# Prompt rows and v rows at other places in VectorE's order, slots of three tiles at earlier blocks

## What is computed

```
q = (x @ w_q).reshape(n, 8, 2, 128)
s1, s2 = q[:, :, 0] @ key1.T, q[:, :, 1] @ key2.T        # 128 keys each
t1, i1 = top_k(s1, 16); t2, i2 = top_k(s2, 16)
top, pos = top_k(all 256 sums t1 + t2, 16)
idx = i1 * 128 + i2 at pos; g = softmax(top)             # 16 of 16384 experts per head
a = sum(u_tab[idx] * x)                                  # one dot product per expert
out = sum(gelu(a) * g * v_tab[idx])
```

## Time and profile before

| | |
|---|---|
| median of three runs | 3657.13 us (3656.3 to 3658.6) |
| the profiled execution | 3659.94 us |
| its span, first to last instruction | 3658.1 us |
| TensorE busy | 3434.4 us, 94% of the span |
| VectorE busy | 2617.4 us, 72% |
| ScalarE, GpSimd busy | 860.4 us, 1728.9 us |
| mean granted TensorE clock | 0.965 |
| DMA | 1263 MB, 345 GB/s over the span |

### The profile page before, as it was taken

How to read it: one execution, slowest core, us unless ns; L and a number is a source line. 1 busy time by engine, 2 the same in 40 slices (tenths; PEclk the granted TensorE clock), 3 DMA queues, 4 the chain that set the end, 5 groups by cost and what they waited for, 6 DMA issues and landing times.

```text
span 3658.1 us, 38233 instructions
## 1 busy us (share of the span) xinstructions
PE 3434.4 (94%) x12478; PEld 2101.6 (57%) x12478; DVE 2617.4 (72%) x6009; ACT 860.4 (24%) x2206; POOL 1728.9 (47%) x1362
## 2 busy tenths in 40 slices
PE   6898989999889999999988988999997999999998
PEld 2555446889778444444435454478886964444443
DVE  0378777898976866666535788689988767666666
ACT  1114311147632000000021160111676310000000
POOL 2035355444635555566300643554456436556661
PEclk9898999999999999999989988999998999999999
DMA  9967588999999999999874965899999999999994
GB/s 361 329 225 264 197 308 326 379 370 370 408 387 377 390 414 413 399 414 412 333 273 153 340 205 194 306 390 375 360 382 408 349 383 401 413 414 398 413 415 170
DMA packets 413989, 1263.48 MB, mean 345 GB/s; under 512 B 36240, under 2 KB 139664, under 8 KB 370784
## 3 DMA queue, kind: packets, MB, share of 16 engines
q0 software_dynamic: 192000, 721.61, 51.0%
q1 hardware_dynamic: 171808, 514.20, 37.0%
q10 hardware_dynamic: 49984, 25.23, 2.3%
HBM read 1174.07 MB, written 86.84 MB: 345 GB/s over the span
## 4 chain that ended last, share of the span: by engine, by line
PE 66%; DVE 14%; DMA 11%; issue 3%; POOL 2%; ACT 2%; SPq 1%; ACTq 0%; DVEq 0%; POOLq 0%
PE P L975 23%; PE P L947 10%; PE P L921 6%; PE V L975 6%; PE O L975 6%; DVE late L1336 4%; PE P L772 4%; DMA gate_d<-hT 3%; PE T L959 3%; POOL ring L686 2%; PE P L755 2%; DMA ring<-in_w_mod_dram 2%; DMA ring<-in_peer_v_dram,eidx 2%; PE O L819 2%; DMA acts_d<-late 1%
## 5 line engine op out<-in xcount | busy, mean ns | idle before, releaser
L686 POOL DMA_INDIRECT ring<-in_peer_u_dram,eidx x768 | 984.3, 1282 | 1011.9 <-DVE ring L1318 644.4
L1318 DVE SCALAR_TENSOR_TENSOR ring<-ring,h 128x1024 f32<-128x1024 f32 x768 | 917.3, 1222 | 159.8 <-DMA ring<-in_peer_u_dram,eidx 152.2
L686 POOL DMA_INDIRECT ring<-in_peer_v_dram,eidx x512 | 704.7, 1376 | 621.1 <-DVE late L1336 348.4
L975 PE MATMUL P<-w_ring,area 128*128 128x512 f32 x2048 | 920.1, 592 | 3.0 <-DVE area L1519 2.2
L947 PE MATMUL P<-hT,w_ring 128*128 128x256 f32 x4096 | 920.5, 383 | 0.0
L947 PEld LDWEIGHTS P<-hT,w_ring 128*128 128x128 f32 x4096 | 777.7, 193 | 102.4
L975 PEld LDWEIGHTS P<-w_ring,area 128*128 128x128 f32 x2048 | 388.6, 190 | 493.8 <-issue 493.7
L1336 DVE SCALAR_TENSOR_TENSOR late<-ring,dots,late 128x1024 f32<-128x1024 f32 x254 | 329.1, 1296 | 55.6 <-DMA ring<-in_peer_v_dram,eidx 38.5
L1336 DVE SCALAR_TENSOR_TENSOR h<-ring,dots,h 128x1024 f32<-128x1024 f32 x254 | 325.7, 1282 | 21.1 <-DMA ring<-in_peer_v_dram,eidx 5.6
L921 PE MATMUL P<-hT,w_ring 128*128 128x128 f32 (+1 forms) x1024 | 287.7, 443 | 2.9 <-issue 2.9
L975 PE MATMUL O<-w_ring,qT 128*128 128x512 f32 x512 | 261.4, 592 | 0.0
(11 more groups left out here) (233 smaller groups left out, 3289.4 us busy)
## 6 DMA issues: line engine op xcount, KB each, us to landing
w_ring<-in_peer_uT_dram SPq DMA_DIRECT2D x128, 1024.0 KB
w_ring<-in_peer_vB_dram SPq DMA_DIRECT2D x128, 1024.0 KB
ring<-in_w_mod_dram POOLq DMA_DIRECT2D x48, 1024.0 KB, 8.2
w_ring<-in_peer_wq_dram SPq DMA_DIRECT2D x64, 512.0 KB, 5.9
h<-acts_d SPq DMA_DIRECT2D x64, 512.0 KB
w_ring<-in_w_in_dram SPq DMA_DIRECT2D x48, 512.0 KB, 3.9
area<-gate_d SPq DMA_DIRECT2D x16, 1536.0 KB
hT<-gate_d SPq DMA_DIRECT2D x16, 1536.0 KB
```

The costliest lines, as they stand in the source:

```text
L686: pool.indirect_dma_start(out=ring[:, b, :], out_offset=None, in_=tables["uv".index(phase)], in_offset=bass.IndirectOffsetOnAxis(ap=eidx[: ...
L975: mm = pe.matmul(bank[ACC[2 * t + half]][:, :], w, uv_ring[:, b // 2 % (WR // 2), b % 2, half * 512:(half + 1) * 512], start=b == 0, stop= ...
L1318: dve.scalar_tensor_tensor(ring[:, b, :], ring[:, b, :], 1.0, h2[:, k, :], ALU.mult, ALU.mult, accum_out=dots[:, k, row:row + 1]).then_inc ...
```

## The change

The prompt rows move: 38 instead of 36 after the input projection, 15 (`WAIT_ROWS`) instead of 8 before the wait for the LayerNorm rows, three instead of two after each of three tiles, and all the other 26 in one run after the last tile; none stand before the key steps. ScalarE's `gelu_dots(0)` moves from j = 7 to j = 3 and VectorE's `expert_weights(0)` from j = 7 to j = 4. The v rows in the key steps stand in three groups: 20 at j = 4, 18 at j = 8 and 18 at j = 12, 56 instead of 52. Beside the search of tile 3 stand 20 v rows (in six steps instead of twelve), to row 76 instead of 72, and 24 rows of tile 1 instead of 16. The `slT` jobs of tiles 3, 4 and 1 move from blocks 43, 75 and 101 to 33, 64 and 97. The chunks of tile 3 begin at block 37 instead of 47 at the same rate; those of tile 4 take 28 blocks from block 66 instead of 23 from 77; those of tile 1 take 20 blocks from 99 instead of 16 from 103. Beside the chunks of tile 1 stand 24 v rows instead of 28, and 12 more come after the last of them, so 16 instead of 28 are left for the v stage. ScalarE's softmax and gelu jobs move with the slots.

```diff
--- before.py
+++ after.py
@@ -57,11 +57,14 @@
 OH_BUFS = 5
 OH_AHEAD = OH_BUFS - 1
 ACT_SIDE = QUAD - 1
-PV_EARLY = 72
-IN_ROWS = 36
-OUT_ROWS = 2
-QUERY_ROWS = 52
-PV_LATE = 100
+QUERY_ROWS = {4: (0, 20), 8: (20, 38), 12: (38, 56)}
+PV_EARLY = 76
+PV_BESIDE = 100
+PV_LATE = 112
+IN_ROWS = 38
+WAIT_ROWS = 15
+OUT_ROWS = 3
+SEARCH_ROWS = 24
 V_DONE = KEYS - 1
 
 SEARCHED_EARLY = 16
@@ -101,7 +104,7 @@
 
 
 
-SLOT_BLOCKS = {43: 3, 75: 4, 101: 1}
+SLOT_BLOCKS = {33: 3, 64: 4, 97: 1}
 
 SEARCH_CHUNKS = 22
 
@@ -111,8 +114,8 @@
 def chunk_block(k, q):
 
     if k == 3:
-        return 47 + q if q < SEARCH_CHUNKS else 70 + (q - SEARCH_CHUNKS) // 2
-    first, blocks = {4: (77, 23), 1: (103, 16)}[k]
+        return 37 + q if q < SEARCH_CHUNKS else 59 + (q - SEARCH_CHUNKS) // 2
+    first, blocks = {4: (66, 28), 1: (99, 20)}[k]
     return first + blocks * q // CHUNKS
 
 
@@ -1114,7 +1117,7 @@
                                            ready(job)[:, :].rearrange("p (c n) -> p c n", c=4), ACT.Copy
                                            ).then_inc(emptied[BANK[job]], 1)
                     for j in range(2 * PH + 1):
-                        if g == "S" and j == 7:
+                        if g == "S" and j == 3:
                             gelu_dots(0)
                         if j < 2 * PH:
 
@@ -1158,11 +1161,11 @@
                                        ).then_inc(emptied[BANK[job]], 1)
                         if b == 18:
                             top_softmax(1)
-                        if b == 41:
+                        if b == 29:
                             top_softmax(3)
-                        if b == 65:
+                        if b == 55:
                             top_softmax(4)
-                        if b == 100:
+                        if b == 96:
                             gelu_dots(1)
                     elif job[0] == "slT":
                         k = job[1]
@@ -1679,7 +1682,7 @@
                     modulation("attended")
                     if latent:
 
-                        prompt_rows(GP)
+                        prompt_rows(WAIT_ROWS)
                     dve.wait_ge(rows_in, (2 * l + (gi + 1)) * 48)
                     for t in range(nt):
                         for n in range(2):
@@ -1688,36 +1691,33 @@
                         if latent and t < nt - 1:
                             prompt_rows(OUT_ROWS)
                     if latent:
-                        prompt_rows(SLOTS - IN_ROWS - 40 - GP - OUT_ROWS * (nt - 1) - 20)
+                        prompt_rows(SLOTS - IN_ROWS - 40 - WAIT_ROWS - OUT_ROWS * (nt - 1))
                     modulation("summed")
                     for j in range(2 * PH):
-                        if latent and j < 5:
-                            prompt_rows(4)
-                        if latent and j == 7:
+                        if latent and j == 4:
                             expert_weights(0)
-                        if latent and j >= 7:
-                            add_rows(0, QUERY_ROWS * (j - 7) // 9, QUERY_ROWS * (j - 6) // 9)
+                        if latent and j in QUERY_ROWS:
+                            add_rows(0, *QUERY_ROWS[j])
                         first_tile_keys(g, j)
                     for step in range(6):
                         choose(tiles[0], step)
 
                 for i in range(2 * PH + 6):
-                    if i < 12:
-                        add_rows(0, QUERY_ROWS + (PV_EARLY - QUERY_ROWS) * i // 12,
-                                 QUERY_ROWS + (PV_EARLY - QUERY_ROWS) * (i + 1) // 12)
+                    if i < 6:
+                        add_rows(0, 56 + 20 * i // 6, 56 + 20 * (i + 1) // 6)
                     else:
-                        dot_rows(1, 16 * (i - 12) // 10, 16 * (i - 11) // 10)
+                        dot_rows(1, SEARCH_ROWS * (i - 6) // 16, SEARCH_ROWS * (i - 5) // 16)
                     choosing(3, i)
                 slots_out(3)
                 for i in range(2 * PH + 6):
-                    dot_rows(1, 16 + ROWS_BESIDE * i // 22, 16 + ROWS_BESIDE * (i + 1) // 22)
+                    dot_rows(1, SEARCH_ROWS + ROWS_BESIDE * i // 22, SEARCH_ROWS + ROWS_BESIDE * (i + 1) // 22)
                     one_hots(3, i)
                     choosing(4, i)
                 slots_out(4)
                 for i in range(CHUNKS - SEARCH_CHUNKS):
                     one_hots(3, SEARCH_CHUNKS + i)
-                    dot_rows(1, 16 + ROWS_BESIDE + i, 17 + ROWS_BESIDE + i)
-                near = 16 + ROWS_BESIDE + CHUNKS - SEARCH_CHUNKS + GP
+                    dot_rows(1, SEARCH_ROWS + ROWS_BESIDE + i, SEARCH_ROWS + ROWS_BESIDE + i + 1)
+                near = SEARCH_ROWS + ROWS_BESIDE + CHUNKS - SEARCH_CHUNKS + GP
                 dot_rows(1, near - GP, near)
                 for i in range(CHUNKS):
                     one_hots(4, i)
@@ -1727,8 +1727,9 @@
                 slots_out(1)
                 for i in range(CHUNKS):
                     one_hots(1, i)
-                    add_rows(0, PV_EARLY + (PV_LATE - PV_EARLY) * i // CHUNKS,
-                             PV_EARLY + (PV_LATE - PV_EARLY) * (i + 1) // CHUNKS)
+                    add_rows(0, PV_EARLY + (PV_BESIDE - PV_EARLY) * i // CHUNKS,
+                             PV_EARLY + (PV_BESIDE - PV_EARLY) * (i + 1) // CHUNKS)
+                add_rows(0, PV_BESIDE, PV_LATE)
 
                 for b in range(KEYS):
                     weights_T(b)
```

## The result

The changed kernel takes 3729.0 us (3725.5 to 3739.9), the kernel before 3656.7 us: a ratio of 1.0216 (95% interval 1.0197 to 1.0235). Forecast were 3671 us with a range of 3634 to 3694. The sign was right, the size was not: +72 us instead of +14, outside the range and beyond the slowest of the rivals (3691). It is the fastest of four executions, so the ledger is 7 us short of the difference of the medians.

The account below looks back on a forecast made before the run. TensorE, busy 94%, was taken as the bound, with DMA traffic close behind in the u stage. +10.2 + 6.7 - 3.0 = +13.9 us on the median of 3657.1 gave 3671 us, own range 3660 to 3684, 8-in-10 range 3634 to 3694.

Parts of the forecast that it names:

- Part 1: Before the first score: two more prompt rows on VectorE's path cost 2.8 us a layer (2.3 to 3.5).
- Part 2: Wait for LN rows: seven more rows fit VectorE's waits and cost zero, or 2 us without the second wait's cover.
- Part 3: Output projection: a third row in each of three tiles makes VectorE 2.55 us later, all on TensorE's path.
- Part 4: 26-row run and gelu at j = 3: ScalarE's late query 3 stalls TensorE, 7.7 us a layer (0.2 to 18).
- starved rival: Run of 26 rows: every gather behind the ring is slow, 50.4 us instead of 40.1; 3691 us in all, chance 0.10.
- lock of the Trainium skill: Run of 26 rows: GpSimd, writing descriptors, can be locked out of a port pair for a whole VectorE instruction.
- Part 5: Slots of tile 3: VectorE has them at 766.5 us as before, so TensorE waits 25 us instead of 4.
- Part 6: Rest of the u stage behind the slots: middle values of 420.6 us (+10.2) and 424.9 us (+6.7) by layer.
- upper end: Stretch behind the slots: DMA traffic of 163.2 MB at the old rate, 427 us and 435.5 us in layer 1.
- sign of being right: Rest of the u stage: TensorE's waits at line 959 for chunks under 13 us a layer.
- Part 7: First v-stage blocks: 16 v rows beside them instead of 28 win 1.5 us a layer.
- sum: Whole kernel: +10.2 + 6.7 - 3.0 = +13.9 us, giving 3671 us.

Follow-up runs that it names:

- gelu4_wait8: Changed kernel with gelu_dots(0) at ScalarE's j = 4 instead of 3 and WAIT_ROWS 8 instead of 15: 3710.9 us, 1.0169 of the kernel before.
- gelu_at_4: Changed kernel with only gelu_dots(0) moved from ScalarE's j = 3 to j = 4: 3717.3 us, 1.0190 of the kernel before.
- search_16: Changed kernel with SEARCH_ROWS 16 instead of 24: 3724.2 us, 1.0185 of the kernel before.
- halved gathers: Tile 1's u rows behind the slots gather 512 instead of 1024 numbers per token: 3699.3 us in the changed kernel, 3604.5 us in the kernel before.
- even spread: Changed kernel with tile 3's last ten chunks one a block instead of two, tile 4's slots at block 69, its chunks in 24 blocks: 3740.4 us.
- late_rows_100: Changed kernel with PV_LATE 100 instead of 112, twelve v rows back beside the v stage's first blocks: 3724.0 us, 1.0193 of the kernel before.
- order_only: Kernel before with only the new places of slots, chunks and ScalarE's softmax and gelu jobs, no row moved: 3713.5 us, 1.0176.
- rows alone: Changed kernel with slots, chunks and ScalarE's softmax and gelu places of the kernel before, row moves kept: 3678.0 us, 1.0084.

## Why the prediction was wrong in size

**Part 1 (+2.8)** was somewhat small. The start of the output projection in layer 0 moves by 0.4 us between the two profiled executions (409.71 to 410.09), but the changed one is the earliest of eight with 38 rows: the middle ones differ by 3.9 us (409.8 and 413.7). In layer 1, from the prompt's last h2 to the projection, they differ by 3.3.

**Part 2 (0) failed.** "Their gathers come late by 1 to 3 us, which the second wait covers": they came late by 3.45, 2.02, 1.45, 1.56 and 1.00 us, 9.5 in all, and the second residual starts 6.8 us later, not 0 to 2. The wait that was to be filled was itself a wait for DMA (the LN rows), whose share was already 0.85 in that window and rises to 0.99. `gelu4_wait8` shows the cost by taking the seven rows away: 6.4 us in layer 0 of the changed kernel, 4.8 against `gelu_at_4` in both layers. That it is the sharing of the engines, and not only that 15 rows are more than the ring's eight, fits the windows but no run separates the two.

**Part 3 (+2.55)** is right: in steady state a tile of 15.17 us where TensorE's takes 14.61 or less; with Part 2 taken away the projection to T3 takes 69.81 us instead of 67.26, and the wait for the last h2 is 12.08 us (`gelu4_wait8`), against 12 forecast. With Part 2 it is 14.07.

**Part 4 (+7.7, 6.8 of it stall)** is right in kind and nearly in size: a stall of 5.54 us at the predicted line, the run of 26 rows in 40.8 us (40.1 forecast from before), ScalarE idle before the gelu; T3 to the u stage grows by 6.3 us. The starved rival (50.4 us for the run) does not hold: the rows came at the old pace. So the lock of the Trainium skill (SBUF — State Buffer, "SBUF: two separate sides") does not make every gather of this run slow: from 487 to 527 us they take 0.93 to 1.99 us on GpSimd. The u stage starts at 626.4, 15.7 us later (13 forecast). The fix of one step gives 8.4 us back.

**Part 5 (slots at 766.5, a wait of 25 us)** had the mechanism and missed the time: 779.9 and 35.9 us. VectorE's wait at keys 3 is 25.09 us (26 forecast) and the pair search starts at 651.0 (648.0 forecast, from a T3 4 us earlier). Then "from there to the slots it took 109.3 us without a wait; now 8 dot rows more, 118.5": it took 128.9. The 20 v rows now stand in six steps instead of twelve, and the u rows follow at once; VectorE waits 9.1 us for rows, where it had not waited. The forecast carried "without a wait" over from an order with half the v rows in a step. (`search_16`, with eight u rows less, takes 115.8 us there: 9.2 us less of work and 2.6 of the waits, and a little more.)

**Part 6 (+10.2, +6.7) is the step that failed most**, with +24.7 and +15.4 us. It took the middle between TensorE's bare time (414.2 us) and the bytes at the old rate (427 and 435.5 us). Measured are 435.8 and 434.3: at the upper end in layer 1, and 9 us beyond it in layer 0, where the bytes were right (435 us x 372 GB/s = 161.8 MB, with 163.2 forecast) but the rate of 382 GB/s did not hold. Its sign of being right came true all the same: TensorE's waits at the chunks are 9.9 and 10.5 us, under 13. The excess over bare time fell from 33 and 41 us to 24 and 23, not to 9 and 13; in layer 0 it is these 9.9 us, 4.7 ahead of the v stage and 2.9 for weights, and the rest goes with the clock, granted at 0.98. "Between these ends nothing in the trace decides" passed over the DMA share of 1.02 and 1.01 through all of the stretch; the spread of the chunks, taken as an argument against that end, changes no byte. The halved gathers showed that their traffic makes the excess, and the even spread that the bunches don't. Bytes over one rate are a near price and no law: `late_rows_100` has the bytes of before, with ten blocks more for TensorE, and takes 429 us. The Trainium skill (DMA: Bandwidth & Descriptors, "Specifications") has beside the ports' 435 GB/s, which the prediction weighed, a limit of about 358 GB/s for one core's share of HBM; the windows lie above it, at 372 to 382 over the stretch and 416 from 702 to 744 us, so it is no ceiling here, and neither figure prices the stretch.

**Part 7 (−1.5 a layer)** is right in one layer. The wait of 1.46 us in the v stage stood only in layer 0, and it is gone. The 761.9 us from the first v block to the prompt's h2 of layer 1, against 763.5 before, show nothing, since the other kernels with the same v rows have 763.3 to 766.7. Against it stand the 6 us a layer that the twelve rows cost in the stretch, 4 of them as a longer wait ahead of the first v block.

**The forecast of a loss** thus stood on its first reason, that VectorE sets the time of the slots and an earlier place in TensorE's order is only a wait; `order_only` shows that alone. Of the sum's miss of 51.6 us, the stretch behind the slots has 23, layer 0 up to the slots 13 (its rows beside the search and before its LN rows), and layer 1's front and slots most of the rest.

## What to carry to other kernels

Moving a job forward in an in-order engine's program helps only if its producer is earlier too; find who sets its time first, and put work into that producer's waits. Where a stretch has a DMA share of 1 over its whole length, price it near its bytes over the measured rate and not by a middle value, and allow some per cent for the rate: it was 364 to 385 GB/s in the kernels here. Spreading the same bytes won nothing. A wait for a DMA hides only part of the work that itself needs more DMA: two rows more cost nothing there, seven cost more than half of their own time.

## What the runs showed of the hardware

- The mixed traffic of gathers, weight blocks and stores runs at 372 to 382 GB/s through 410 to 435 us in the two kernels, and at 364 (`late_rows_100`) to 385 GB/s (rows alone) in the others with full gathers, all at a share of 0.99 to 1.03, with 389 and 416 GB/s in windows of 18 and 42 us.
- With half-size gathers the DMA engines show a share of 0.95 to 0.97 at 326 to 337 GB/s: 10 to 13% fewer GB/s lower the share by 4 to 7% only, so the share alone does not say how many bytes there is room for. The profile counts 64 packets fewer for each halved gather.
- Beside the LN rows' loads, a gather took a median of 11.5 us from issue to landing (5.3 to 13.3), where its issue on GpSimd took 0.94 us. From 651 to 780 us the median of the u rows' gathers was 15.9 us.
